# The latent heads of the last two layers: parts without position on two halves of the partitions, rotary parts on 32-row groups, one embedding

## What is computed

```python
qc = jnp.einsum('bsr,rc->bsc', rms_norm(cq, c_qn), c_wuq).reshape(bsz, s_len, C_HEADS, C_NOPE + C_ROPE)
qc_nope = qc[..., :C_NOPE]
qc_rope = apply_rope(qc[..., C_NOPE:], rope_mla[0], rope_mla[1])
kv = jnp.einsum('bsr,rc->bsc', rms_norm(ckv, c_kvn), c_wukv).reshape(bsz, s_len, C_HEADS, C_NOPE + C_V)
kc_nope = kv[..., :C_NOPE]
kc_rope = apply_rope(ckr[:, :, None, :], rope_mla[0], rope_mla[1])[:, :, 0, :]
...
        s = (jnp.einsum('bqhd,bkhd->bhqk', qn_b, k_nope)
             + jnp.einsum('bqhr,bkr->bhqk', qr_b, k_rope)).astype(jnp.float32) * scale
```

## Time and profile before

| | |
|---|---|
| median of 3 runs | 1965.51 us (1963.92 to 1968.25) |
| the profiled execution's own time | 1968.18 us |
| its span | 1966.4 us |
| mean granted clock of TensorE | 0.973 of full |
| TensorE busy | 1878.5 us, 96% of the span |
| VectorE, ScalarE, GpSimd busy | 817.7, 782.1, 597.8 us |
| shares of the chain that ended last | PE 90%, DVE 4%, ACT 3%, POOL 2% |
| DMA | 141.54 MB, 72 GB/s in the mean |
| layer 0's heads (first logits to first O) | 1482.29 to 1592.40 us, PE busy 102.56 of 110.11 |
| layer 1's heads | 1795.78 to 1906.28 us, PE busy 102.96 of 110.50 |

### The profile page before, as it was taken

How to read it: one execution, slowest core, us unless ns; L and a number is a source line. 1 busy time by engine, 2 the same in 40 slices (tenths; PEclk the granted TensorE clock), 3 DMA queues, 4 the chain that set the end, 5 groups by cost and what they waited for, 6 DMA issues and landing times.

```text
span 1966.4 us, 23067 instructions
## 1 busy us (share of the span) xinstructions
PE 1878.5 (96%) x9756; PEld 1489.7 (76%) x9756; DVE 817.7 (42%) x1338; ACT 782.1 (40%) x1286; POOL 597.8 (30%) x182
## 2 busy tenths in 40 slices
PE   8998899989999999999899999989998999998997
PEld 5777799988788888887788888877674468765456
DVE  7663545653123212102562035135635644625653
ACT  5974465443333333223332122224335533334541
POOL 3331432032232333444254434433420005322001
PEclk9998899989999999999899999989999999999999
DMA  5110000122323332232132323223110012211001
GB/s 198 65 65 0 1 1 21 45 91 75 135 96 107 97 112 85 87 107 86 45 127 86 107 86 107 86 86 137 67 65 22 1 43 99 86 63 44 1 1 43
DMA packets 28992, 141.54 MB, mean 72 GB/s; under 512 B 2871, under 2 KB 7351, under 8 KB 14936
## 3 DMA queue, kind: packets, MB, share of 16 engines
q1 hardware_dynamic: 18944, 122.94, 17.4%
q10 hardware_dynamic: 9944, 17.12, 2.6%
HBM read 134.80 MB, written 5.24 MB: 71 GB/s over the span
## 4 chain that ended last, share of the span: by engine, by line
PE 90%; DVE 4%; ACT 3%; POOL 2%; issue 1%; DMA 0%; POOLq 0%; SPq 0%; DVEq 0%; ACTq 0%
PE bank L403 54%; PE bank L1032 8%; PE bank L607 5%; PE bank L414 4%; PE bank L1977 3%; PE bank L1998 3%; PE bank L1984 2%; PE bank L1437 1%; ACT w_part L361 1%; PE bank L1413 1%; PE bank L655 1%; PE bank L1926 1%; PE bank L792 1%; ACT WK L2107 1%; PE bank L1068 1%
## 5 line engine op out<-in xcount | busy, mean ns | idle before, releaser
L403 PE MATMUL bank<-x_part,w_part 128*128 128x512 f32 x3264 | 764.8, 394 | 0.6 <-DVE x_part L571 0.6
L403 PEld LDWEIGHTS bank<-x_part,w_part 128*128 128x128 f32 x3264 | 614.6, 189 | 135.0 <-issue 6.1
L2424 POOL TENSOR_TENSOR w_part<-RAW,w_part 128x2048 fp32r<-128x2048 f32 (+1 forms) x90 | 402.9, 4480 | 819.4 <-ACT w_part L361 819.4
L2424 POOL TENSOR_TENSOR w_part<-WK,w_part 128x2048 fp32r<-128x2048 f32 (+1 forms) x30 | 125.1, 4169 | 376.7 <-ACT w_part L361 376.7
L361 ACT ACTIVATE w_part<-RAW 128x2048 fp32r<-128x2048 f32 (+1 forms) x90 | 166.5, 1851 | 175.7 <-PE bank L403 138.3
L403 PE MATMUL bank<-f_part,w_part 128*128 128x512 f32 x768 | 174.4, 389 | 0.0
L403 PEld LDWEIGHTS bank<-f_part,w_part 128*128 128x128 f32 x768 | 144.1, 188 | 29.9
L1032 PE MATMUL bank<-WK 128*128 128x128 f32 (+1 forms) x1056 | 125.0, 279 | 5.3 <-DVE WK L1265 3.7
L1032 PEld LDWEIGHTS bank<-WK 128*128 128x128 f32 (+1 forms) x1056 | 119.7, 194 | 7.6 <-DVE WK L1265 4.0
L1977 PE MATMUL bank<-WK 64*128 64x512 f32 (+3 forms) x256 | 81.7, 593 | 9.7 <-ACT STAT L2093 9.7
L903 DVE SCALAR_TENSOR_TENSOR WK<-bank,COL,WK 128x510 f32<-128x510 f32 (+1 forms) x96 | 71.6, 749 | 46.3 <-ACT WK L863 43.7
(11 more groups left out here) (281 smaller groups left out, 2392.8 us busy)
## 6 DMA issues: line engine op xcount, KB each, us to landing
RAW<-wts SPq DMA_DIRECT2D x84, 1024.0 KB, 4.8
WK<-wts SPq DMA_DIRECT2D x24, 1024.0 KB, 4.8
WK<-scratch ACTq DMA_DIRECT2D x16, 256.0 KB, 2.7
RAW<-wts SPq DMA_DIRECT2D x6, 512.0 KB, 3.4
WK<-wts SPq DMA_DIRECT2D x6, 512.0 KB, 3.5
scratch<-WK ACTq DMA_DIRECT2D x4, 768.0 KB, 3.3
WK<-xT SPq DMA_DIRECT2D x4, 512.0 KB, 5.8
WK<-xT ACTq DMA_DIRECT2D x1, 2048.0 KB, 12.7
```

Of the source, the lines that this page charges most:

```text
L403: mm = pe.eng.matmul(b[:, :], W[w][:, k, c:c + P], src[x][k], start=start and k == 0 and n == 0, stop=stop and k == kn - 1 and n == 2)
L2424: eng.tensor_tensor(low_part(i), raw_part(i), high_part(i).bitcast(F32), ALU.subtract).then_inc(w_split, 1)
```

## The change

The latent queries come in three tiles of 128 rows instead of four of 96: two with the 64 rows without position of two heads each, on the lower and the upper half of the partitions, and one with the 32 rotary rows of all four heads (in the order 0, 2, 1, 3). The keys without position come in two tiles of 128 rows. The weight of the key's rotary part stands in its projection four times, so that it lies in four 32-row groups without copies. `qrot` and its `rope` are one each. The logits of a latent pair are two matmuls over 64 rows, one on each half, and then two over 32 rows that add to the same banks (rows 0 and 64 for heads 0 and 1, rows 32 and 96 for heads 2 and 3).

```diff
             b = job((L, "krot"))
-            E.matmul(b[0:96, :], tab("rc")[0:96, 0:96], CL[0:96, 3, :], start=True, stop=True).then_inc(*pe.did(("pe", (L, "krot"))))
+            E.matmul(b[:, :], tab("ra"), CL[:, 3, :], start=True, stop=True).then_inc(*pe.did(("pe", (L, "krot"))))
...
-            for h in range(4):
-                b = job((L, "uq", h))
-                E.matmul(b[0:96, :], UQ[:, 0, h * 96:(h + 1) * 96], CL[:, 0, :], start=True, stop=False)
-                E.matmul(b[0:96, :], UQ[0:64, 1, h * 96:(h + 1) * 96], CL[0:64, 1, :], start=False, stop=True).then_inc(*pe.did(("pe", (L, "uq", h))))
-            for h in range(4):
-                b = job((L, "uk", h))
-                E.matmul(b[0:64, :], UKV[:, h * 64:(h + 1) * 64], CL[:, 2, :], start=True, stop=True).then_inc(*pe.did(("pe", (L, "uk", h))))
+            for j in (2, 0, 1):
+                b = job((L, "uq", j))
+                E.matmul(b[:, :], UQ[:, 0, j * P:(j + 1) * P], CL[:, 0, :], start=True, stop=False)
+                E.matmul(b[:, :], UQ[0:64, 1, j * P:(j + 1) * P], CL[0:64, 1, :], start=False, stop=True).then_inc(*pe.did(("pe", (L, "uq", j))))
+            for j in range(2):
+                b = job((L, "uk", j))
+                E.matmul(b[:, :], UKV[:, j * P:(j + 1) * P], CL[:, 2, :], start=True, stop=True).then_inc(*pe.did(("pe", (L, "uk", j))))
...
-            for h in range(4):
-                pe.wait_ge(*at((L, "cqc", h)))
-                b = job((L, "qrot", h))
-                E.matmul(b[0:96, :], tab("rc")[0:96, 0:96], CQ[0:96, h, :], start=True, stop=True).then_inc(*pe.did(("pe", (L, "qrot", h))))
+            pe.wait_ge(*at((L, "cqc", 2)))
+            b = job((L, "qrot"))
+            E.matmul(b[:, :], tab("ra"), CQ[:, 2, :], start=True, stop=True).then_inc(*pe.did(("pe", (L, "qrot"))))
...
-                E.matmul(b[:, 0:len(ks) * P], qf[:, t * P:(t + 1) * P], kf[:, ks[0] * P:(ks[-1] + 1) * P], start=True, stop=True)\
-                    .then_inc(*pe.did(("pe", (L, "l", n, t))))
+                mm = E.matmul(b[:, 0:len(ks) * P], qf[:, t * P:(t + 1) * P], kf[:, ks[0] * P:(ks[-1] + 1) * P], start=True, stop=kind != "C")
+                if kind != "C":
+                    mm.then_inc(*pe.did(("pe", (L, "l", n, t))))
+                return b
+
+            def roped(n, t, b):
+                r = slice(32 * ROPED.index(heads[n][6]), 32 * ROPED.index(heads[n][6]) + 32)
+                E.matmul(b[:, :], CQ[r, 2, t * P:(t + 1) * P], CL[r, 3, :], start=False, stop=True).then_inc(*pe.did(("pe", (L, "l", n, t))))
...
-                    logits(2 * m, t)
-                    logits(2 * m + 1, t)
+                    two = [logits(n, t) for n in (2 * m, 2 * m + 1)]
+                    if heads[2 * m][5] == "C":
+                        roped(2 * m, t, two[0])
+                        roped(2 * m + 1, t, two[1])
...
-            dve.wait_ge(*dve.last())
-            for h in range(4):
-                V.tensor_copy(CK[64:96, h, :], CL[64:96, 3, :]).then_inc(*dve.did())
...
-            for h in range(4):
-                dve.wait_ge(*at((L, "cqc", h)))
-                dve.wait_ge(*dve.last())
-                rope(CQ[:, h, :], (L, "qrot", h), tab("cc"), tab("cs"), SQL[:, 3, :], 96, None, [])
+            dve.wait_ge(*at((L, "cqc", 2)))
+            dve.wait_ge(*dve.last())
+            rope(CQ[:, 2, :], (L, "qrot"), tab("cc"), tab("cs"), SQL[:, 3, :], P, None, [])
```

More of the change, by code:

```diff
@@ L49 @@
 PAIRED = [0, 3, 1, 4, 2, 5]
+ROPED = [0, 2, 1, 3]
 MIXED = [12, 13, 6, 9, 0, 3, 14, 15, 7, 10, 1, 4, 8, 11, 2, 5]
@@ L157, in shape_constants @@
     for n in range(2):
[L158 to L164, removed]
+        tabs.append(np.concatenate([mla[n]] * 4, 0))
+    tabs += [half_turn(P, 32), half_turn(P, 64)]
     k = np.arange(3 * P)[None, :]
@@ L171 @@
 TAB = dict(ac=(0, 512), asn=(512, 512), bc=(1024, 512), bs=(1536, 512), cc=(2048, 512), cs=(2560, 512),
-           ra=(3072, 128), rb=(3200, 128), rc=(3328, 128), win=(3456, 384))
-NTAB = 3840
+           ra=(3072, 128), rb=(3200, 128), win=(3328, 384))
+NTAB = 3712
 def build(nc, xT, cols, base, gdnc, tabs, wgate, relb, sel, small, wts, out, scratch, old):
@@ L1867, in attention_heads @@
             for h in range(4):
-                out.append((CQ[0:96, h, :], CK[0:96, h, :], 256 + 64 * h, 768 + 64 * h, SC_C, "C", h))
+                half = slice(64 * (h % 2), 64 * (h % 2) + 64)
+                out.append((CQ[half, h // 2, :], CK[half, h // 2, :], 256 + 64 * h, 768 + 64 * h, SC_C, "C", h))
             return [out[i] for i in (12, 13, 6, 7, 0, 1, 14, 15, 8, 9, 2, 3, 10, 11, 4, 5)]
@@ L2077, in lay_act @@
             ahead(f"L{l}V", 0)
-            for h in range(4):
-                act.wait_ge(*at(("pe", (L, "uq", h))))
-                A.activation(CQ[0:96, h, :], ps((L, "uq", h))[0:96, :], ACT.Copy, scale=SC_C).then_inc(*act.did((L, "cqc", h), free=(L, "uq", h)))
-            for h in range(4):
-                act.wait_ge(*at(("pe", (L, "uk", h))))
-                A.activation(CK[0:64, h, :], ps((L, "uk", h))[0:64, :], ACT.Copy).then_inc(*act.did(free=(L, "uk", h)))
+            for j in (2, 0, 1):
+                act.wait_ge(*at(("pe", (L, "uq", j))))
+                A.activation(CQ[:, j, :], ps((L, "uq", j))[:, :], ACT.Copy, scale=SC_C).then_inc(*act.did((L, "cqc", j), free=(L, "uq", j)))
+            for j in range(2):
+                act.wait_ge(*at(("pe", (L, "uk", j))))
+                A.activation(CK[:, j, :], ps((L, "uk", j))[:, :], ACT.Copy).then_inc(*act.did(free=(L, "uk", j)))
             for t in range(TT):
@@ L2206, in lay_dve @@
                      [(L, "ropes")] if i == 7 else [])
-            for i, m in enumerate((P, 64, P, 96)):
+            for i, m in enumerate((P, 64, P, P)):
                 scaled(CL[:, i, :], (L, "C", i), m, (L, "krc") if i == 3 else (L, "ccp", i))
@@ L2215, in lay_dve @@
             dve.wait_ge(*at((L, "krc")))
-            rope(CL[:, 3, :], (L, "krot"), tab("cc"), tab("cs"), SQL[:, 3, :], 96, None, [])
-            dve.wait_ge(*dve.last())
-            for h in range(4):
-                V.tensor_copy(CK[64:96, h, :], CL[64:96, 3, :]).then_inc(*dve.did())
+            rope(CL[:, 3, :], (L, "krot"), tab("cc"), tab("cs"), SQL[:, 3, :], P, None, [])
             def grow(j):
@@ L2500, in lay_out @@
         get[f"L{l}B"] = np.concatenate([part(l, "bq", 384, PAIRED), part(l, "bk", 128)], 1)
-        get[f"L{l}C"] = np.concatenate([part(l, "cq", 192), zeros64, part(l, "ckv", 128), zeros64, part(l, "ckr", 32), zeros64[:, :32]], 1)
+        get[f"L{l}C"] = np.concatenate([part(l, "cq", 192), zeros64, part(l, "ckv", 128), *[part(l, "ckr", 32)] * 4], 1)
         get[f"L{l}V"] = np.concatenate([part(l, "av", 128), part(l, "bv", 128)], 1)
@@ L2537, in lay_out @@
     for l in range(LAYERS):
-        uq, ukv = A(c_w_uq_2)[l], A(c_w_ukv_2)[l].reshape(P, 4, 2, 64)
+        uq, ukv = A(c_w_uq_2)[l].reshape(192, 4, 96), A(c_w_ukv_2)[l].reshape(P, 4, 2, 64)
+        uq = np.concatenate([uq[:, :, 0:64].reshape(192, 256), *[uq[:, h, 64:96] for h in ROPED]], 1)
         small[l, :, 0:384] = uq[:P]
```

## The result

The changed kernel is slower: median 1973.06 us against 1965.90 of the kernel before (15 runs each), ratio 1.0034 with a 95% interval of 1.0023 to 1.0045. I had forecast 1962.1.

What follows compares the result with a forecast made beforehand. TensorE's own time was taken as the bound (busy 96% of 1966.4 us). Terms -12.8 + 8.7 + 0.75 = -3.4 against the profiled 1968.18 gave 1964.8, for the median 1962.1; range 1956.5 to 1970.

Steps and rivals of the forecast that it cites:

- What goes: Latent projections on TensorE: fewer passes in uq (-2.06), uk (-1.78) and qrot (-2.57), -6.4 us a layer, -12.8 in all.
- What comes, pair m=3: Later latent pair in the heads: its four steps with the new 64- and 32-row matmuls cost +1.6 us a layer.
- in turn: Rival, heads: two 32-row groups don't overlap, rotary pair 1.90 us instead of 1.06, +13.4 in all, 1975.5; chance 0.12.
- in order: Rival, heads: only head 0's second rotary pass and head 1's first overlap, +6.9 us, 1969.0; chance 0.06.
- cheaper rotary pass: Rival, heads: rotary pair needs no shape change, 0.86 us, -3.2; with some lateness caught, 1957 to 1959; chance 0.23.
- The bank rotation: Start of O in layer 1: TensorE waits for VectorE's out(7) to read bank 6, +0.75 us, once.
- What comes, pair m=0: First latent pair, beginning of the heads: slower steps, partly at low clock, make TensorE go on later, +2.7 us a layer.
- 1.13 steps fit: Beginning of the heads: new steps of 4.24 us each at half clock, before full clock returns at about 1487.
- +2.7: First latent pair: TensorE goes on after ScalarE's copy at 1497.4 instead of 1494.72, a delay that stays, each layer.
- low clock for longer: Rival, beginning of the heads: low stretch lasts 3 us more a layer, half of it lost, 1965.1; chance 0.11.

## Why the prediction was wrong

- **What goes** was right: 6.35 and 6.31 us a layer for 6.4. Nothing else became late: TensorE waits for no weights there.
- **What comes, pair m=3** was right: 17.10 us for its four steps (1520.25 to 1537.35) for 15.51 before, +1.59 against +1.6. The price of a 32-row pair, which I called the weakest point, was exact, and so the rivals "in turn" and "in order" are out, and so is the cheaper rotary pass. The Trainium skill, page "TensorE: Matmul & The Clock Gate", Part 3, has matmuls start and end strictly in program order; taken pass by pass, as my rival took it, the trace doesn't show that, since the first passes of both heads start together at 1521.31, ahead of both second ones.
- **The bank rotation** was right in place and size: 0.89 for 0.75 us, in layer 1 alone.
- **What comes, pair m=0** is the step that failed, in one number: I carried the low stretch over as it was, up to "4.8 us after TensorE's start", so that "1.13 steps fit" in it. It lasted 23.8 us in layer 0 and 16.9 in layer 1. The term "+2.7" measured +8.6 up to the third transposes of layer 0 and +7.0 in layer 1 (19.73 from first logits to third transposes for 12.70), and +9.9 by the time layer 0's later latent pair starts (1475.38 to 1520.25 for 1482.29 to 1517.29). At full clock it is 2.5: the mechanism that I followed was right and the clock under it wrong. Against the forecast this one term is 5.9 + 4.3 us at the third transposes and 1.3 more behind them in layer 0, 11.5 in all; the 1.7 us of clock at the end of layer 1's heads, which came by chance, hide a part of it in the spans.
- **The rival "low clock for longer"** named the cause, but with 3 us more of it in place of 17 and 10, and a chance of 0.11. I argued against it from the A pairs, whose 64 rows run at full clock; they overlap on both halves and work all rows, so they said nothing about 32 of 128. And they run at full clock already: what keeps a clock up is no evidence of what brings it back. With the measured 17 and 10 us in place of 3, and half of them lost as that rival had it, its time would have been some 13.5 us over the forecast; it came 11 over.
- The range ended at 1970 because passes in turn, the one large slower case, were left out of it, and the low clock stood in it with 3 us.

## What to carry to other kernels

Count a packed matmul by the rows at work at once, not by its passes: behind an idle stretch on TensorE, matmuls that work half of the rows, and what follows them, can stay at half clock for 20 us without a gap, and the price of a small tile is then twice its passes. At full clock the same matmuls did not bring it down. Where a kernel must start such a phase after a wait, fill the wait with full-height matmuls into a bank that nobody reads. And when an edit saves in one stage and pays in the next, try to cut it at the seam: here the packed projections and the old logits together beat both kernels.

## What the runs showed of the hardware

- With 3.0 to 4.8 us of idleness ahead of the heads the granted clock fell to 0.50 in every layer; with the 2.2 us at their end it fell in some layers and not in others. Ahead of the heads it came back after a low stretch of 3.3 to 6.7 us where the first matmuls were 96 rows high or 64-row pairs on both halves, and of 17 to 24 us where they worked half of the rows or fewer for at least a part of the time: 64 rows in turn (23.7, 20.4), 32 rows in turn (20.3, 20.4), and 64-row pairs in alternation with overlapped 32-row pairs (23.8, 16.9; with the banks moved 23.7, 16.9; with the shorter idleness 16.9, 20.4). From the first logits on TensorE had no gap in these long stretches of the changed kernel (busy 23.72 of 23.80 us in layer 0). The Trainium skill, page "TensorE: Matmul & The Clock Gate", Part 1, says that the throttled state is the default and activity releases it; here being busy without a gap was not enough. How the chip counts rows, these runs don't show.
- Half-row work held a low clock down but did not lower a full one: with the wait filled, the same alternation of 64- and 32-row pairs ran at 1.00 (38.3 us from 1461.7), and so did the later latent pair in the changed kernel (1.06 and 1.05 us a pair).
- Two fp32 matmuls on different row groups overlap over both of their passes, for 64 rows and for 32: 1.06 us a pair for 512 columns. Two 64-row pairs behind one another take 0.96 each, a 64-row and a 32-row pair 1.06 and 1.05.
- ScalarE's copy of a 64-row half to other partitions took 0.59 us, one of 128 rows in place 0.59 to 0.60.
